# A retention layer's state update for eight samples: full-array products against groups of four 32-row array tiles

## What is computed

```python
def retention_chunk(q, k, v, S):
    ...
    scores = jnp.einsum('bhld,bhmd->bhlm', q, k) * dmask
    out = (jnp.einsum('bhlm,bhmv->bhlv', scores, v)
           + jnp.einsum('bhld,bhdv->bhlv', q, S) * q_decay[:, :, None])
    S_new = S * s_decay[:, None, None] + jnp.einsum('bhmd,bhmv->bhdv', k * k_decay[:, :, None], v)
    return out, S_new
```

## Time and profile before

| | us |
|---|---|
| median of 3 runs | 1781.61 (1780.8 to 1782.35) |
| span of the profiled execution, first to last instruction | 1778.7 |
| TensorE busy | 1728.7 (97%) |
| DVE busy | 1066.0 (60%) |
| ACT busy | 713.4 (40%) |
| GpSimd busy | 171.9 (10%) |
| mean granted TensorE clock | 0.990 |

### The profile page before, as it was taken

One profiled execution on the slowest core, in us unless ns is written; L12 is line 12 of the kernel. 1 busy time (PEld: TensorE's weight loads), 2 busy tenths in 40 slices (PEclk: granted clock), 3 DMA queues, 4 the chain that ended last, 5 costly groups with the idle time before them and its releaser, 6 DMA issues. The chain is left out here.

```text
span 1778.7 us, 31973 instructions
## 1 busy us (share of the span) xinstructions
PE 1728.7 (97%) x11196; PEld 1676.5 (94%) x11196; DVE 1066.0 (60%) x1656; ACT 713.4 (40%) x1118; POOL 171.9 (10%) x245
## 2 busy tenths in 40 slices
PE   8999999999999999999999999979999999999995
PEld 8999999999999999999999999859999999999994
DVE  6666566656656656656665666795444444454465
ACT  4543443443353353344344344454333333333333
POOL 1010001001001001000000100440000000000243
PEclk9999999999999999999999999989999999999998
DMA  8547647647646655754864764535444444444442
GB/s 322 171 165 256 218 146 260 239 155 240 244 152 237 231 196 197 253 212 141 279 218 164 245 241 142 202 110 175 145 142 153 152 143 153 153 142 143 143 155 83
DMA packets 93420, 334.23 MB, mean 188 GB/s; under 512 B 10560, under 2 KB 12752, under 8 KB 93328
## 3 DMA queue, kind: packets, MB, share of 16 engines
q1 hardware_dynamic: 72976, 257.65, 42.1%
q0 software_dynamic: 20352, 75.23, 13.1%
HBM read 292.32 MB, written 40.52 MB: 187 GB/s over the span
## 5 line engine op out<-in xcount | busy, mean ns | idle before, releaser
L1120 PE MATMUL proj<-x_hi,w_hi 128*128 128x322 f32 (+2 forms) x2560 | 776.3, 314 | 25.3 <-DVE x_lo L986 12.2
L1121 PE MATMUL proj<-x_lo,w_hi 128*128 128x322 f32 (+2 forms) x2560 | 773.4, 313 | 0.0
L731 DVE TENSOR_TENSOR w_lo<-w_raw,w_hi 128x1024 fp32r<-128x1024 f32 x416 | 512.9, 1240 | 208.8 <-ACT w_hi L490 192.4
L490 ACT CAST w_hi<-w_raw 128x1024 fp32r<-128x1024 f32 x416 | 434.2, 1049 | 444.1 <-PE proj L1121 280.5
L1120 PEld LDWEIGHTS proj<-x_hi,w_hi 128*128 128x128 f32 x2560 | 482.9, 189 | 35.2 <-issue 19.0
L1121 PEld LDWEIGHTS proj<-x_lo,w_hi 128*128 128x128 f32 x2560 | 483.7, 189 | 6.9
L1125 PE MATMUL proj<-x_hi,w_lo 128*128 128x322 f32 (+2 forms) x2560 | 435.1, 312 | 0.3 <-DVE w_lo L731 0.3
L1125 PEld LDWEIGHTS proj<-x_hi,w_lo 128*128 128x128 f32 x2560 | 395.9, 189 | 0.6 <-DVE w_lo L731 0.6
L1278 PE MATMUL proj<-qk_or_z,w_hi 128*128 128x322 f32 x512 | 156.2, 317 | 2.8 <-DVE residual L812 2.7
L1279 PE MATMUL proj<-qk_or_z,w_hi 128*128 128x322 f32 x512 | 153.1, 311 | 0.0
L802 DVE TENSOR_TENSOR s_lo<-te_for_q_or_prompt_state,s_hi 128x512 fp32r<-128x512 f32 x128 | 85.4, 688 | 74.6 <-ACT s_hi L529 74.6
(11 more groups left out here) (161 smaller groups left out, 1446.5 us busy)
## 6 DMA issues: line engine op xcount, KB each, us to landing
w_raw<-w_head SPq DMA_DIRECT2D x256, 512.0 KB, 4.4
w_raw<-w_conv SPq DMA_DIRECT2D x128, 512.0 KB, 3.3
state_update<-s_in POOLq DMA_DIRECT2D x64, 512.0 KB, 6.2
te_for_q_or_prompt_state<-s_in SPq DMA_DIRECT2D x64, 512.0 KB, 4.6
s_out<-state_update POOLq DMA_DIRECT2D x64, 512.0 KB, 3.7
w_raw<-w_cout SPq DMA_DIRECT2D x32, 512.0 KB, 3.4
s_prompt<-te_for_q_or_prompt_state POOLq DMA_DIRECT2D x8, 512.0 KB, 6.6
head_table<-tables POOLq DMA_DIRECT2D x8, 441.0 KB, 3.6
```

Of the source, the lines that this page charges most:

```text
L490: act.copy(w_hi[:, i % SPL, :], w_raw[:, i % RAW, :]).then_inc(w_h.sem, 1)
L731: TT(w_lo[:, i % SPL, :], w_raw[:, i % RAW, :], f(w_hi[:, i % SPL, :]), ALU.subtract).then_inc(w_l.sem, 1)
L1120: mm(bank[:, 0:n], wh[:, k, :], rhs_h(k), start=(first and k == 0), stop=False)
L1121: x = mm(bank[:, 0:n], wh[:, k, :], rhs_l(k), start=False, stop=False)
```

## The change

The stacks are filled by transfers from SBUF to SBUF that SP issues, of rows that exist already: block m = 2 of `k_hi`, `k_lo`, `v_hi`, `v_lo` (token rows 256 to 335: 16 of the prompt, then 64 of the samples). Twelve transfers for k after the load of chunk 17 and twelve for v after that of chunk 22. Row 4n + c of a stack is copy c of token n, so rows 32r to 32r + 31 hold the 8 tokens of sample r (or 4 + r) in four copies. The mask, `k_of_sample`, the staging tile, its copies and its 12 transposes go. One group of `kv_multiply` is four products of 32 rows each, for four samples, into banks 1 to 4; four groups in a head. Four further transfers of each twelve stack the last 16 prompt rows the same way (64 rows, the other 64 zero), so that one product takes the place of three in the prompt's state. The updates on DVE stay 16 in a head, by a table of their own, and GpSimd's stores and reloads follow the new order (samples 0 to 3, then 4 to 7). In the first LayerNorm the square sum uses bank `qs`.

```diff
-KV_AT = {19: 0, 20: 1, 21: 2, 22: 3, 24: 4, 25: 5, 26: 6, 27: 7, 29: 8, 30: 9, 32: 10, 33: 11, 34: 12, 36: 13, 37: 14,
-         39: 15}
-KB_AT = {18: 0, 20: 1, 22: 2, 24: 3, 27: 4, 30: 5, 33: 6, 36: 7}
+KV_AT = {25: 0, 29: 1, 33: 2, 37: 3}
+KU_AT = {26 + t: t for t in range(16)}
+C_HI = (1, 1, 0, 0), (1, 0, 1, 0)
...
+            def stack_rows(hi, lo, of, st, ps, sem):
+
+                for c in range(4):
+                    rows = hi if C_HI[of][c] else lo
+                    for f in range(2):
+                        t0 = META + f * (NSAMP // 2)
+                        sp.dma_start(st[c:P:4, f, :].bitcast(F32), rows[t0:t0 + NSAMP // 2, 2, :].bitcast(F32)).then_inc(sem, 16)
+                    sp.dma_start(ps[META * c:META * c + META, :].bitcast(F32), rows[0:META, 2, :].bitcast(F32)).then_inc(sem, 16)
+
             def head_loads(h, first):
                 for i in range(first, CPH):
                     load_chunk(0, h, CPH, i, w_head[h, i])
+                    if i == 17:
+
+                        sp.wait_ge(kn_l.sem, kn_l.at(h, 3))
+                        stack_rows(k_hi, k_lo, 0, k_st, k_ps, ks_in.sem)
+                    if i == 22:
+                        sp.wait_ge(vn_l.sem, vn_l.at(h, 3))
+                        stack_rows(v_hi, v_lo, 1, v_st, v_ps, vs_in.sem)
                     if i in SA_AT:
...
-            def kv_multiply(h, t, back):
-                b = t // 2
-                if t < 2:
-
-                    pe.wait_ge(vs_made.sem, vs_made.at(h, t + 1))
-                else:
-                    pe.wait_ge(s_new.sem, s_new.at(h, t - 1, back))
-                pe.wait_ge(kb_made.sem, kb_made.at(h, b + 1, back))
-                mm(bank_r[3 + t % 2][:, :], k_b[:, b % 2, P * (t % 2):P * (t % 2) + P], v_st[:, b // 4, :],
-                   start=True, stop=True).then_inc(kv_done.sem, 1)
+            def kv_multiply(h, g, back):
+
+                f, d = g // 2, g % 2
+                if g:
+                    pe.wait_ge(s_new.sem, s_new.at(h, 4 * g, back))
+                for r in range(4):
+                    rows = slice(32 * r, 32 * r + 32)
+                    x = mm(bank_r[1 + r][:, :], k_st[rows, f, P * d:P * d + P], v_st[rows, f, :], start=True, stop=True)
+                x.then_inc(kv_done.sem, 1)
...
-                        for m in range(3):
-                            rows = KEY[m][1]
-                            c = slice(P * d, P * d + P)
-                            x = three(bank_q[:, :], k_hi[0:rows, m, c], k_lo[0:rows, m, c],
-                                      v_hi[0:rows, m, :], v_lo[0:rows, m, :], m == 0, m == 2)
-                        x.then_inc(st_done.sem, 1)
+                        else:
+                            pe.wait_ge(kn_l.sem, kn_l.at(h, 3))
+                            pe.wait_ge(ks_in.sem, ks_in.at(h, ks_in.per))
+                            pe.wait_ge(vs_in.sem, vs_in.at(h, vs_in.per))
+                        c = slice(P * d, P * d + P)
+                        for m in range(2):
+                            three(bank_q[:, :], k_hi[:, m, c], k_lo[:, m, c], v_hi[:, m, :], v_lo[:, m, :], m == 0, False)
+                        mm(bank_q[:, :], k_ps[:, c], v_ps[:, :], start=False, stop=True).then_inc(st_done.sem, 1)
```

More of the change, by code:

```diff
@@ L404, in less_mean, with rest_of_states @@
                     pool.tensor_tensor(blk(k, n), blk(k, n), cols(ln_m, n), ALU.subtract).then_inc(n_t[n].sem, 1)
+            def rest_of_states(h, more):
+                store(h, 2, 1)
+                reload(h, 1, 1)
+                store(h, 3, 1)
+                reload(h, 2, 1)
+                reload(h, 3, 1)
+                for b in range(4, NB):
+                    store(h, b, 1)
+                    if more and b > 4:
+                        reload(h, b - 1, 1)
+                if more:
+                    reload(h, NB - 1, 1)
             def head(h, first, last):
                 if not first:
-                    for b in range(KV_NEXT, NB):
-                        store(h, b, 1)
-                        reload(h, b - 1, 1)
+                    rest_of_states(h, True)
                 pool.wait_ge(y_ve.sem, y_ve.at(h))
@@ L454, in _ @@
             pool.dma_start(csi[:, :, :, :], cs_in).then_inc(cw_in.sem, 16)
-            for b in range(KV_NEXT, NB):
-                store(HEADS, b, 1)
+            rest_of_states(HEADS, False)
             norm_zero(1)
@@ L551, in side @@
                         act.copy(kt_hi, k_raw).then_inc(k_h.sem, 1)
[L552 to L557, removed]
-                            act.copy(st_k[:, d, :, 1, :], src).then_inc(sk_h.sem, 1)
                     if 10 <= i <= 16 and i % 2 == 0:
@@ L619, in side @@
                         z_round(0, 1, 2)
-                    for back, b in due(KB_AT, i, first):
-                        kb_make(h, b, back)
                 for i in range(CPH):
@@ L678, in conv @@
                         round_chunk(HEAD_CH, j, CPE, i)
-                    if done:
-                        for back, b in due(KB_AT, i, last=True):
-                            kb_make(HEADS, b, back)
                     if done and i >= 4:
@@ L925, in side @@
                         out_read(i - 25)
-                    for back, t in due(KV_AT, i - 1, first):
+                    for back, t in due(KU_AT, i, first):
                         kv_update(h, t, back)
@@ L1010, in conv @@
                     if done:
-                        for back, t in due(KV_AT, i - 1, last=True):
+                        for back, t in due(KU_AT, i, last=True):
                             kv_update(HEADS, t, back)
@@ L1056, in conv_all @@
                 if done:
-                    for back, t in due(KV_AT, CPE - 1, last=True):
-                        kv_update(HEADS, t, back)
+                    for i in (CPE, CPE + 1):
+                        for back, t in due(KU_AT, i, last=True):
+                            kv_update(HEADS, t, back)
                 conv_end(j)
@@ L1440, in head_tables @@
         con[[j, NSAMP + j], 2 * P + META + j] = 1.0
-    con[0:META, 3 * P] = 1.0
-    for b in range(4):
-        con[:, 3 * P + 1 + b] = (np.arange(P) % 32) // DSEQ == b
     return tables, trig, con
```

140 lines of the change are left out of this document (36 added, 104 removed).

## The result

| | before | after |
|---|---|---|
| median of the runs, us | 1781.43 (1780.8 to 1782.35, 4 runs) | 1800.68 (1798.83 to 1802.13, 4 runs) |
| span of the profiled execution, us | 1778.7 | 1800.6 |
| TensorE busy, us | 1728.7 | 1721.4 |
| mean granted TensorE clock | 0.990 | 0.982 |

A forecast was written before the change was run, and what follows sets the result against it. TensorE's instruction list was taken to bound the eight heads. Terms -32.2 + 11.8 + 6.4 + 0.7 = -13.3 us took the profiled 1778.7 to 1765.4; plus 2.9 for the median, the forecast was 1768.3 us, range 1749 to 1785.

The forecast's parts named there:

- What leaves TensorE's list: In each head, vanished stack transposes, prompt-state products and update products save 4.03 us, 32.2 us for eight heads.
- The groups: Four row-tile groups per head, each in place of one 0.23 us product, add 1.48 us a head, 11.8 in all.
- G: TensorE's price of one group of four 32-row products, taken as 0.60 us, bounded by 0.23 and 1.46.
- What moves on SP's queue: Twelve issues delay sample 5's state load, so TensorE waits after chunk 14: 0.8 us a head, 6.4 in all.
- GpSimd's stores and reloads: Between updates 18 us apart in a head, storing and reloading a buffer takes 9.9 us and costs nothing.
- a sign that the prediction named as "wrong": In the timeline, DVE waiting for a reload of `state_update` would show the forecast to be wrong; no size given.
- The last head's 0.7: In the last head, whose output projection DVE already bounds, one more update falls in and adds 0.7 us.
- The sum: Over the whole kernel, savings and costs together give -13.3 us, from 1778.7 to 1765.4 for the profiled execution.
- (c): On SP's queue, sample 5's state comes late and TensorE waits 5 us a head: 1802 us, chance 0.07.
- (a): In the groups, tiles run wholly together at 0.23 us and SP is in time: 1750 us, chance 0.25.
- (b): Groups on TensorE cost as much as they save, 1.1 us each: 1784 us, or 1778 without the wait; chance 0.12.
- (d): Waits open at half of the other removed product places in the heads, losing about 10 us: 1779 us, chance 0.11.

The follow-up runs named there:

- k_late: The changed kernel with the twelve k transfers issued after the load of chunk 21 instead of chunk 17: 1766.66 us, 0.9916 of before.
- state_first: The changed kernel with sample 5's state load issued ahead of the twelve k transfers behind chunk 17's load: 1768.00 us, 0.9923 of before.
- conv_last: k_late with conv block 0's groups after chunks 3 and 6, DVE's updates moved along, sample 1's reload earlier in the last head: 1762.04 us, 0.9893.

## Why the prediction was wrong, point by point

- **What leaves TensorE's list** (4.03 us a head): right. The eight transposes gave 1.34 - 0.47 = 0.87, the four 0.45 (0.40 forecast), the prompt's state 0.93 (0.92), the eight places of the update 0.23 each, the places in the output projection nothing, as the earlier trace rows were read.
- **The groups** (+1.48 a head): right in size, G 0.63 for 0.60, so 1.6. The make-up was wrong: not four weight loads of 0.11 and a tail of 0.16, but 0.23 for all four together and 0.39 for going in and out; that 0.60 came so near is luck. With list and groups together heads 1 to 6 of k_late take 141.01 us against 143.51: 2.50 less, 2.55 forecast.
- **"What moves on SP's queue"** (+6.4): the step that failed, by its size. The mechanism was named in full, to the place after chunk 14 and the releaser. The issue was put at 0.42, between 0.33 and the 0.53 of a row at the start; it is 0.64 from start to start. Twelve times 0.22 is 2.6 us, and they fall on the far side of the slack: six issues cost nothing, twelve cost 2.8 to 4.9 us in each head, 3.3 in the mean, where 0.8 was taken. The prediction's own chain gave 1.7; with 0.64 for an issue (+2.6) and the landing of 3.3 to 3.8 us that the traces show in place of 4.7 (-1.2), it gives 3.1, and of the step from 1.7 down to 0.8 only 0.5 had a row behind it. The row of issues that follow one another was at hand and was the nearer one: at its 0.53 the same chain gives 3.1 us a head, and no gain is left. Taking the middle was the choice that went wrong, and the low bound on the wait (2.5 at most) followed from it. The load of chunk 18 leaves 5.0 us later, not 3, and costs nothing, as state_first shows.
- **What the wait does to the clock**: not in the sum at all, and no reason was given for leaving it out. 8.8 us of the 35 that the late state costs come from it.
- **GpSimd's stores and reloads** (nothing): a sign that the prediction named as "wrong" did appear, DVE waiting for a reload, though its cost stayed small. The kernel before has no such wait. Ten of its eleven occurrences in the kernel after stand at chunks 2, 3 and 5 of the heads; TensorE lost some 1.2 us by them in all, at chunk 5. GpSimd itself waits 137.7 us for stores ahead of its reloads. The 9.9 us for store and reload were too low: they land after 4.2 and 7.3 us in the median now, and a store after up to 11.0, where 6.8 was the most before. DVE's wait in the kernel after (us in total, times, longest):

```profile
DVE state_update L736 <- DMA state_update<-s_in: 18.0, 11, 4.9
```

- **The last head's 0.7**: wrong, by a place. In conv block 0 it is 6.3: the prediction said the stages after the LayerNorm were unchanged, but two of the four groups of the last head fall into them, and a group waits for four banks at once where a product waited for one.
- **The start**: 0.8 us more in this trace. k_late has it in one of its two traces (0.8) and not in the other (0.1), so it is no effect of the change that these runs show.
- **The sum**: forecast -13.3, in the traces +21.9. Of the 35.2 between them the wait makes 19.9, the clock 8.8, conv block 0 5.6, the start 0.8.
- **The rivals.** (c) had the mechanism; its number is luck. It gave 1802 from 0.53 for each issue, a landing of 7 and 5 us of wait; the measured 0.64, 3.3 to 3.8 and 3.3, with the clock and conv block 0 on top, arrive at nearly the same. Its argument against, that the twelve carry only 320 KB, counted bytes where issues were the cost. That k_late, at 1766.7, lies within 2 us of 1768.3 is luck too: it has no wait, for which 6.4 were in the sum, and loses 7.2 in conv block 0, for which 0.7 were. conv_last, with neither, is the fair comparison: 1762.0, where the sum without the wait gives 1761.9. (a) and (b) are out by G, (d) by the places in the heads, which kept their gain.

## What to carry to other kernels

Count what is added to a queue in issues, not bytes, price each at the highest issue-to-issue distance in the trace (0.53 here, and even that was low), and compare the sum with the slack of the first load behind it; where slack and delay are close, move the block (here from chunk 17 to 21, 34 us) before anything else. Small row-tile groups pay their 0.39 us for the mode once, so put as many tiles as possible behind one another; replacing full products by lone groups gains little in itself, and here the gain came from the transposes and products that vanished. A group that fills several banks at once needs all of them read: check every stage it falls into, the last one too.

## What was not expected of the hardware

- A row of issues of 16 KB to 32 KB from SBUF to SBUF on SP: 0.59 us each, 0.64 from start to start, whatever the partitions they write; a 512 KB load 0.58 when it follows such a row by 0.04 us, 0.33 when it stands alone.
- A wait that made TensorE 2.8 to 4.9 us late brought 3.4 or 6.8 us at 1.2 GHz in five of eight heads of the kernel after, and none in the other three.
- One 32-row tile costs TensorE as much as four beside one another, 0.62 and 0.63 us among full-array products.
- A kernel that only adds transfers far from the turn of its loop showed about 2.5 us of "issue" at three of those turns, and was 7.5 us slower. Two 16 KB code packets stand ahead of each long turn, one ahead of each of the others; that they are the cause was not tested.
